# Reordered scans, one projection before the first gates, and turns around the last residual, in an encoder layer

## What is computed

```python
proj = x @ w_in + b_in
u_lru, g_lru, q, k, v, gate_lru, gate_attn = jnp.split(proj, SPLIT_IDX, axis=-1)
u = depthwise_conv(u_lru, w_lru_conv, b_lru_conv, LRU_CONV_PAD)
h_fwd = rg_lru_scan(u, ...)              # forward over positions
h_bwd = flip(rg_lru_scan(flip(u), ...))  # backward
#   r = sigmoid(u @ w_a + b_a), i = sigmoid(u @ w_x + b_x), in 8 blocks of 160 channels
#   a = exp(8 r log_sigmoid(lam)),  h[t] = a[t] h[t-1] + sqrt(1 - a^2) * i * u
y_lru = ((h_fwd + h_bwd) * gelu(g_lru)) @ w_lru_out
y_attn = windowed_gqa(q, k, v, rel_table, attn_sink) @ w_attn_out
mix = (sigmoid(gate_lru) * y_lru + sigmoid(gate_attn) * y_attn) @ w_o + b_o
x = layer_norm(ALPHA * x + mix, ln1_g, ln1_b)
hu = depthwise_conv(x @ w_up + b_up, w_ffn_conv, b_ffn_conv, FFN_CONV_PAD)
val, gt = jnp.split(hu, 2, axis=-1)
return layer_norm(ALPHA * x + (gelu(gt) * val) @ w_down + b_down, ln2_g, ln2_b)
```

## Time and profile before

| | us |
|---|---|
| median of 3 runs (2743.85 to 2744.9) | 2744.3 |
| the profiled execution, whole | 2745.17 |
| its span in the profile | 2743.4 |

### The profile page before, as it was taken

One profiled execution on the slowest core, in us unless ns is written; L12 is line 12 of the kernel. 1 busy time (PEld: TensorE's weight loads), 2 busy tenths in 40 slices (PEclk: granted clock), 3 DMA queues, 4 the chain that ended last, 5 costly groups with the idle time before them and its releaser, 6 DMA issues.

```text
span 2743.4 us, 32010 instructions
## 1 busy us (share of the span) xinstructions
PE 2659.9 (97%) x11898; PEld 2193.1 (80%) x11898; DVE 1486.2 (54%) x1780; ACT 768.5 (28%) x1053; POOL 653.2 (24%) x332
## 2 busy tenths in 40 slices
PE   8998999999999999999999999989999999999998
PEld 6786888888788877888888888878788778888886
DVE  6799754334504568644545464667742414644445
ACT  3565713313400022010101111148932301211112
POOL 3554532232133622434243332310000000000000
PEclk9999999999999999999999999999999999999999
DMA  6554554444596823435343433456656693544554
GB/s 216 198 196 157 200 184 157 173 161 168 201 375 230 314 87 129 157 133 180 129 181 124 177 129 147 148 210 219 227 199 229 218 355 134 207 184 187 198 199 166
DMA packets 168544, 519.94 MB, mean 190 GB/s; under 512 B 13255, under 2 KB 40135, under 8 KB 166384
## 3 DMA queue, kind: packets, MB, share of 16 engines
q1 hardware_dynamic: 113536, 422.02, 42.6%
q10 hardware_dynamic: 54896, 96.39, 9.9%
HBM read 303.13 MB, written 206.32 MB: 186 GB/s over the span
## 4 chain that ended last, share of the span: by engine, by line
PE 83%; DVE 10%; DMA 3%; ACT 3%; issue 1%; SPq 0%; ACTq 0%; DVEq 0%
PE ps L877 49%; PE ps L1218 12%; PE ps L1045 8%; PE ps L1139 4%; PE ps L927 3%; PE ps L1028 2%; PE ps L1078 1%; DMA gate_in<-gate_dram 1%; DMA W<-w_split 1%; PE ps L1065 1%; PE ps L930 1%; PE ps L1207 1%; DVE tau L1801 1%; DVE tau L1791 0%; DVE acc L2082 0%
## 5 line engine op out<-in xcount | busy, mean ns | idle before, releaser
L877 PE MATMUL ps<-XH,W 128*128 128x512 f32 x4224 | 1206.0, 391 | 26.9 <-DVE XL L1746 11.7
L877 PEld LDWEIGHTS ps<-XH,W 128*128 128x128 f32 x4224 | 794.8, 188 | 203.9 <-issue 19.6
L877 PE MATMUL ps<-XL,W 128*128 128x512 f32 x2112 | 710.0, 390 | 0.0
L877 PEld LDWEIGHTS ps<-XL,W 128*128 128x128 f32 x2112 | 397.9, 188 | 82.4
L1218 PE MATMUL ps<-W,HH 128*128 128x512 f32 x1152 | 310.1, 389 | 1.5 <-DVE HL L2065 1.5
L1218 PEld LDWEIGHTS ps<-W,HH 128*128 128x128 f32 x1152 | 216.1, 188 | 46.8 <-DVE HL L2065 1.9
L761 POOL TENSOR_SCALAR W<-raw 128x1024 fp32r<-128x1024 f32 (+2 forms) x72 | 91.4, 1270 | 566.8 <-PE ps L877 301.7
L1045 PE MATMUL ps<-XH,W 128*128 128x512 f32 x672 | 216.4, 393 | 0.0
L827 POOL TENSOR_SCALAR W<-raw 128x1024 fp32r<-128x1024 f32 x72 | 86.8, 1205 | 536.8 <-PE ps L877 228.8
L762 POOL TENSOR_TENSOR W<-raw,W 128x1024 fp32r<-128x1024 f32 (+2 forms) x72 | 205.6, 2855 | 6.0
L828 POOL TENSOR_TENSOR W<-raw,W 128x1024 fp32r<-128x1024 f32 x72 | 190.3, 2643 | 6.0
(11 more groups left out here) (205 smaller groups left out, 3341.8 us busy)
## 6 DMA issues: line engine op xcount, KB each, us to landing
w_split<-W SPq DMA_DIRECT2D x131, 1024.0 KB, 6.2
W<-w_split SPq DMA_DIRECT2D x130, 1024.0 KB, 6.8
raw<-w_mlp SPq DMA_DIRECT2D x72, 512.0 KB, 4.2
raw<-w_qkv_mix SPq DMA_DIRECT2D x28, 512.0 KB, 3.7
w_split<-W SPq DMA_DIRECT2D x8, 1280.0 KB, 12.3
W<-w_split SPq DMA_DIRECT2D x8, 1280.0 KB, 8.3
gate_dram<-mix_out ACTq DMA_DIRECT2D x16, 512.0 KB, 2.7
gate_in<-gate_dram ACTq DMA_DIRECT2D x16, 512.0 KB, 6.2
```

What stands on the lines that cost most here:

```text
L877: last = nc.tensor.matmul(bank(group, c), lhs(wl, k), rhs(xl, k, c), start=(k == 0 and n == 0), stop=(k == nk - 1 and n == 2))
```

## The change

Three places are touched.

**Half.** `decay_steps` is divided (`gate_inputs` and `decay_steps`), and `recur` too (`scans` and `output`). At the transition from half 0 to half 1, DVE now runs: `gate_inputs` and `decay_steps` of (0, REST_TILE), a wait for the sigmoids of block 4, `convolve(1, 1)`, the scans of (0, REST_TILE), `gate_inputs` and `decay_steps` of (1, 0), the split of (1, 1), the scans of (1, 0), then `output(0, REST_TILE)`, `convolve(1, 2)`, `output(1, 0)`. ACT issues the store of (0, REST_TILE) behind the roots and the takes of (1, 0) instead of ahead of its roots. The second square of half 1 goes to `ur[0]` and no longer waits for the moves out of `sig_rest`. A block's first sigmoid waits for one scan instead of two.

**Border.** In `q == 1`, `("g", 0, 0)` comes ahead of `("gates", 0, 0)` in the order of slabs and products; ACT's order of takes stays. The row before the last gets a store semaphore of its own, and ACT waits for the other five only.

**Norm.** Five turns of the first half lie within the last token tile, three between the first parts of `up_half(0, 0)`; the last three take-backs and splits of that half come behind the last tile's norm on ACT and behind its residual on DVE. The products that need them, and the turns of the second half, follow `up_half(1, 0)`'s first five parts.

```diff
-BACK_AT = ((0, 2, 2, 2, 2, 0, 0, 0), (0, 0, 1, 1, 1, 1, 2, 2))
+BACK_AT = (0, 0, 2, 0, 2, 0, 1, 0)
+EARLY_BACK = 5
+TURNS_LATE = (0, 2, 1, 1, 1, 1)
...
+        def order_of(q):
+            return order_lru if q == 0 else order_lru[:3] + [order_lru[4], order_lru[3]] + order_lru[5:]
...
-            return out_stored[0 if tt in (0, SEQS[q] // P - 1) else 1]
+            last = SEQS[q] // P - 1
+            return out_stored[0 if tt in (0, last) else 2 if tt == last - 1 else 1]
...
-            return (sq, sig_rest)[d][:, 0:T]
+            return (sq, ur[0] if h else sig_rest)[d][:, 0:T]
...
-                    for e in order_lru[AHEAD if q else 0:]:
+                    for e in order_of(q)[AHEAD if q else 0:]:
...
                     pe.wait_ge(res_taken[q], nt - 1)
-                    up_half(0, 0)
+                    for k in range(EARLY_BACK):
+                        up_half(0, 0, range(k, k + 1))
+                        if k < KD - EARLY_BACK:
+                            turn_back(0, EARLY_BACK + k)
                     pe.wait_ge(res_taken[q], nt)
-                    up_half(1, 0)
-                    up_half(0, 1).then_inc(slab_done, 1)
-                    up_half(1, 1).then_inc(slab_done, 1)
+                    up_half(1, 0, range(EARLY_BACK))
+                    late = [(n, k) for n in range(2) for k in range(EARLY_BACK, KD)]
+                    made = 0
+                    for (n, k), turns in zip(late, TURNS_LATE):
+                        for kk in range(made, made + turns):
+                            if kk == 0:
+                                pe.wait_ge(normed[q], nt)
+                            turn_back(1, kk)
+                        made += turns
+                        up_half(n, 0, range(k, k + 1))
+                    for kk in range(made, KD):
+                        turn_back(1, kk)
+                    up_half(0, 1, range(KD)).then_inc(slab_done, 1)
+                    up_half(1, 1, range(KD)).then_inc(slab_done, 1)
...
                                 if last is not None:
-                                    act.wait_ge(scan_done[q], 2 * last + 4)
+                                    act.wait_ge(scan_done[q], 2 * last + (4 if m else 3))
...
-                            if h and jj == 0:
-                                store_y(act, q, T, 0, REST_TILE)
                             if h == 0 and jj == HALF - 1:
                                 take("u", 1, REST_TILE)
                             roots(h, jj)
...
                                 for e in behind_gates(h, jj):
                                     take(*e)
+                            if h and jj == 0:
+                                store_y(act, q, T, 0, REST_TILE)
...
                     for tt in range(nt):
                         if tt == nt - 1:
-                            take_back(0)
+                            take_back(0, range(EARLY_BACK))
...
+                    take_back(0, range(EARLY_BACK, KD))
...
+                            r_i = [side(z, jj, T) for z in sig]
+                            if blk == HALF:
+                                output(0, REST_TILE, gelu_gr[:, 0:T])
+                                convolve(1, 2)
+                                output(1, 0, side(gelu_g, 0, T))
+                                continue
...
                         if h == 0:
+                            r_i = [side(z, 0, T) for z in sig]
+                            dve.wait_ge(gate_evac[q], 5 * HALF + 5 + gate_banks(T) - 1)
                             convolve(1, 1)
-                        recur(h, REST_TILE, r_i[0:2], r_i[2:4], gelu_gr[:, 0:T], split_next if h == 0 else (lambda: None))
+                            scans(0, REST_TILE, rests[0:2], rests[2:4])
+                            gate_inputs(1, 0, r_i[2:4], u[0])
+                            decay_steps(1, 0)
+                            split_next()
+                            scans(1, 0, r_i[0:2], r_i[2:4])
...
                         if tt == nt - 1:
-                            split_back(0)
+                            split_back(0, range(EARLY_BACK))
                         add_residual(tt)
-                    split_back(1)
+                    split_back(0, range(EARLY_BACK, KD))
+                    split_back(1, range(KD))
```

More of the change, by code:

```diff
@@ L425, in build @@
         out_ready = PerSeq("out_ready")
-        out_stored = [sem(f"out_stored{i}") for i in range(2)]
+        out_stored = [sem(f"out_stored{i}") for i in range(3)]
         def ln_stat(t):
@@ L697, in _ @@
                 last_gates = None
-                for n, (kind, h, jj) in enumerate(order_lru):
+                for n, (kind, h, jj) in enumerate(order_of(1)):
                     s = first_slab(1, "lru") + n
@@ L908, in gates @@
                     def gates(h, jj):
-                        n = slab_at[("gates", h, jj)]
+                        n = slab_of(q, ("gates", h, jj))
                         blk = HALF * h + jj
@@ L1192, in up, with up_half @@
                         project(n % 2, T, "mlp", n, g=g)
-                    def up_half(n, side):
+                    def up_half(n, side, part):
                         at = side * TH
                         dst = ps[:, 2 * n + at // CH, at % CH:at % CH + TH]
[L1197 to L1204, removed]
+                        if part.start == 0:
+                            slab_in(q, "mlp", n)
+                        for k in part:
                             pe.wait_ge(x1_split[q], KD * side + k + 1)
@@ L1366, in decays @@
                             if d and jj < REST_TILE and not is_short(T):
-                                act.wait_ge(rest_moved[q], 64 * (HALF * h + jj + 2))
-                            A1(square(d, T), r[d], ACT.Square).then_inc(decay_done[q], 1)
+                                if h:
+                                    act.wait_ge(input_gated[q], REST_TILE + 1)
+                                else:
+                                    act.wait_ge(rest_moved[q], 64 * (jj + 2))
+                            A1(square(d, h, jj, T), r[d], ACT.Square).then_inc(decay_done[q], 1)
                     def roots(h, jj):
@@ L1623, in normalise_token_tile, with take_back @@
                            bias=stat[:, 4:5]).then_inc(normed[q], 1)
-                    def take_back(half):
-                        for k in range(KD):
+                    def take_back(half, part):
+                        for k in part:
                             g = half * KD + k
@@ L1686, in _ @@
                     if q + 1 == len(SEQS):
-                        for k in range(2):
+                        for k in range(3):
                             act.wait_ge(out_stored[k], 16 * out_count(q)[k])
@@ L1790, in decay_steps, with scans @@
                             tau_d = tau[n % 2][d][:, 0:T]
-                            tell(V.scalar_tensor_tensor(out=tau_d, in0=square(d, T), scalar=1.0, in1=tau_d, op0=ALU.add, op1=ALU.mult),
-                                 q_ready[q], 2 * n + d + 1)
-                    def recur(h, jj, r, i, gate, between=lambda: None):
+                            tell(V.scalar_tensor_tensor(out=tau_d, in0=square(d, h, jj, T), scalar=1.0, in1=tau_d,
+                                                        op0=ALU.add, op1=ALU.mult), q_ready[q], 2 * n + d + 1)
+                    def scans(h, jj, r, i):
                         n = 5 * h + jj
@@ L1801, in recur, with output @@
                             tell(V.tensor_tensor_scan(o, a, b, 0.0, ALU.mult, ALU.add), scan_done[q], 2 * n + d + 3)
+                    def output(h, jj, gate):
+                        n = 5 * h + jj
+                        tau_j = [t[:, 0:T] for t in tau[n % 2]]
                         order(V.tensor_tensor(tau_j[0], tau_j[0], tau_j[1], ALU.add))
-                        between()
                         dve.wait_ge(proj_evac[q], gelu_at[("g", h, jj)] + 1)
@@ L1834, in _ @@
                                 split_channels(1, REST_TILE)
-                            recur(h, jj, r_i[0:2], r_i[2:4], side(gelu_g, jj, T))
+                            scans(h, jj, r_i[0:2], r_i[2:4])
+                            output(h, jj, side(gelu_g, jj, T))
                             if jj < HALF - 1 and blk + 2 < BLOCKS:
@@ L2015, in add_residual, with split_back @@
                         scale_and_shift(ln_stat(tt % 4), norm_ready[q], tt + 1)
-                    def split_back(half):
+                    def split_back(half, part):
                         at = slice(half * TH, (half + 1) * TH)
-                        for k in range(KD):
+                        for k in part:
                             g = half * KD + k
```

50 lines of the change are left out of this document (29 added, 21 removed).

## The result

| | before | after |
|---|---|---|
| median of 14 runs each, us | 2744.94 (2743.85 to 2748.33) | 2751.39 (2747.26 to 2754.89) |
| the profiled execution, whole | 2745.17 | 2748.74 |
| its span | 2743.4 | 2746.9 |

The ratio is 1.0021, with a 95% interval of 1.0014 to 1.0028: about 6 us slower by these times, clear of the interval but small. The forecast was 2746.3, its range 2737 to 2752. The same kernel in a later set of runs gave 2748.85 against 2745.28, ratio 1.0014 (1.0005 to 1.0023), or 3.6 us slower.

The account below looks back on a forecast made before the run. PE was taken to bound the kernel, at work 2660 of 2743.4 us. Terms -1.1 + 2.4 - 4.8 - 2.7 + 0.9 = -5.3, plus clock +7.3, gave +2.0 on 2744.3: 2746.3 us, range 2737 to 2752.

Parts of the forecast that it names:

- Rival 1: All places: the found waits don't bind and the change does what its order suggests; -27, 2717 us; chance 0.12.
- Rival 2: New waits: PE's clock doesn't fall behind waits of 4 to 5 us; -5.3, 2739.0 us; chance 0.15.
- rival 3: New waits: clock falls behind all four as long as at the border, 2.8 each; +5.9, 2750.2 us; chance 0.15.
- Half, first sequence: Wait before block 5's first sigmoid: PE resumes at 243.5 to 245.5 against 245.59; gain 0.1 to 2.1, taken -1.1.
- The value of the one-scan wait: Half, first sequence: the looser wait for one scan is worth nothing behind the store of y(0, REST).
- Border: Start of second sequence: u_stack moves ready earlier, PE then waits 4.8 us for a gelu before g(0, REST); -4.8.
- the 9.9 that the filled gap was said to promise: Border: gain promised by the filled gap and its clock, where the forecast took -4.8 instead.
- Norm, first: First sequence's norm: residual starts 4.6 earlier, but turn 7 waits 6.0 us for an ACT take; -2.7 (-3.6 to -0.6).
- t + 8.3: First norm: when turn 7 of the second half comes, t being its first turn; part of POOL's split still falls there.
- Norm, second: Second sequence's norm: turn 7 waits 4.3 us in place of 1.65; +0.9 (0.5 to 1.2).
- Half, second: Second sequence's half: PE resumes at 1939.3 instead of 1936.90, with a new wait of 4.2 us; +2.4.
- The clock's total: Behind four new waits: low PE clock costs 1.5 for three and 2.8 for the 6.0 us one; +7.3, bounds 0 and 11.2.

Follow-up runs that it names:

- three moves: Changed kernel with y(0, REST)'s store behind block 5's sigmoids, turn 7 behind the second half's first five parts, second sequence's first gelu taken before the gates' sigmoids; 2728.24 us.
- norm alone: Kernel before with only the norm's part of the change; 2746.51 us against 2745.28, ratio 1.0002.
- border alone: Kernel before with only the border's part of the change; 2746.97 us against 2745.28, ratio 1.0006.
- turn late: Changed kernel with turn 7 of the norm's first half moved behind the first five parts of the second; 2746.24 us against 2745.22 for before.
- half alone: Kernel before with only the half's new order; 2749.37 us against 2745.28, ratio 1.0017.
- moves first: Three moves, with SP's fetch of the second sequence's sixth slab held until the moves into u_stack have landed; 2727.23 us against 2745.31 for before.
- store behind: Changed kernel with ACT's store of y(0, REST) moved from behind block 4 to behind block 5's four sigmoids; 2738.82 us against 2745.22 for before.
- both scans: Store behind, with the first sigmoid again waiting for both scans of the block before instead of one; 2742.50 us against 2745.00 for before.
- no own semaphore: Three moves, without the semaphore of its own for the last row but one; 2728.69 us against 2745.31 for before.
- norm out: Three moves, with the norm's part as in the kernel before; 2731.07 us against 2745.31 for before.

## Why the prediction was right, and where it was not

The time lies inside the range, 5.1 over the forecast by the first median and 2.5 by the second. By the trace it is closer still, +3.5 against +2.0, but in part by luck: the places that the sum names came out 4.2 us above it together, and what it doesn't name took 2.7 back. The mechanism was read rightly at all five places: the half keeps its wait with the store right ahead of the table load; g(0, REST) waits 4.7 (predicted 4.8); turn 7 waits 5.5 and 4.2 (6.0 and 4.3); the second half waits 3.7 and resumes at 1939.18 (1939.3). Rival 1, that the waits don't bind, falls with them. Rival 2, no clock, falls in this execution, in which all four windows are low; rival 3, 11.2 us for them, was too much by 3, though its time, 2750.2, is nearer the first median than the forecast is. What was mis-sized, term by term:

- **Half, first sequence**, -1.1 against +1.1. PE resumes at 245.25, in before's time 246.0 (this kernel began 0.8 us early), behind the upper end of 245.5. The scans end at 239.52, also 0.8 early, so at 240.3: the upper end of 238.2 to 240.2. POOL's subtraction held one DVE operation, as in the earlier trace rows: the scan that began at 231.57 ended 2.15 us behind it, of its own 2.29. That is the Trainium skill's rule in SBUF — State Buffer, section "SBUF: two separate sides", by which the two exclude each other for a whole instruction; the trace agrees, and with it the end at 240.2 was the one to take, not the middle. The issue of the store, about 0.35 of ACT's queue, was counted in the second sequence and forgotten in the first. And the clock behind this wait, 1.9 us lost before and 2.6 now, had no term at all.
- **The value of the one-scan wait.** "Worth nothing behind it" was right, as the store stood; what followed from it, that moving one store a few instructions down is worth 10 us, was not drawn.
- **Border**, -4.8 + 1.5 against -0.1. The take started 1.7 earlier and not 2.35. Then the moves into u_stack: the forecast had PE's gates follow the projection at 1836.1, and they began at 1838.14 behind a DMA. ACT now issues the moves while SP's weight fetches are in flight; that this slows them is what the run with the held fetch shows, in the version with the three moves. The clock took 2.4, not 1.5. The moves, a start of the last wait 0.2 later, and the clock make 2.0 + 0.2 + 0.9 = 3.1 of the 3.2 missed. And the 9.9 that the filled gap was said to promise is 9.6 by its own rows (1855.8 - 1846.2), which changes no term.
- **Norm, first**, -2.7 + 2.8 against -1.3. The clock is right to the tenth (2.8). The turns of the second half end 7.2 us after the first (t + 8.3 taken), since none of POOL's subtractions fell there: the third ended at 1029.28, 2.4 before the first of these turns.
- **Norm, second**, +0.9 + 1.5 against +2.3: right to 0.1, term by term. PE went on at 2335.61, in before's time 2334.3, as forecast; the eight parts behind took 1.6 us more than at full speed; and from the second half's first turn (2340.25) to the end it was 10.95, where 11.0 was taken. The clock loss came through whole, as it did in the second execution (+2.4).
- **Half, second**, +2.4 + 1.5 against +4.2: right within 0.3. The 4.2 us taken for its wait is not worked out in the forecast: from the old start, 1936.90 - 2.56, to 1939.3 it would be 5.0. It measured 3.73, since PE stopped later.
- **Not in the sum**: the start, -0.8 and -1.3 in the two executions of the changed kernel, attention 1, +0.8 in both, and attention 2, -2.6 and -3.0. The last was put at nothing since no instruction changes there.

The clock's total, +7.3 for four waits, was near the 8.0 measured, but as a sum of unequal errors. The rule of TensorE: Matmul & The Clock Gate, section "HAM oscillation — how this bites in real kernels", in the Trainium skill, that waits between groups of matmuls bring the array back at half clock each time, fits all four. Behind shorter waits, at the second half, the rows of this case show both: 1.00 behind 2.56 us (before) and 2.54 (norm alone), 0.51 behind 2.57 (border alone).

**What stays open.** In the first set of 14 runs the median is 6.4 over before, the profiled execution only 3.6, and single times reach 2754.9; in the second set they reach 2752.7. The profile is of one execution, and no profile here is of a time above 2750. What differs between the profiles at places that have the same code is the clock behind a wait and the length of attention 2, both below; that they make the spread of the times too is not shown. Why attention 1 is 0.5 to 0.8 longer in every kernel with the new half (2.2 in turn late) was not tried.

## What to carry over

When an operation is moved later on one engine, look up what waits for its result on the others, and what is queued behind that wait: a store that costs 0.33 us to issue held ACT, and through it PE, for 6 us. A freed wait is worth something only down to the next one in the same queue, so write out all the waits at a place before counting a gain, and move the blocking ones together: the three small moves turned a change that costs 4 to 6 us into one that wins 17. Count the clock behind each new wait as well: at the changed kernel's second norm all of it came through.

## What the chip showed beyond that

**The clock is not a function of the wait.** Waits of 2.57 and 2.56 us in the same place were followed by granted clocks of 0.51 and 1.00; the half's wait of 11.6 us in the first sequence by 0.53 over 5.5 us in the changed kernel and 0.74 in turn late, whose code there is the same. That is 1.2 us, and all of the difference between their first halves in the table.

**Attention 2 differs by up to 4.6 us with no instruction changed.** From 1950 to 2316 us of before the kernels took from 4.1 us less to 0.5 us more. It is not a give-back of what was gained ahead of it: of the kernels that came to it 5 to 17 us early, some kept its length (three moves, moves first) and some made it 1 to 3 us shorter (store behind, both scans, no own semaphore, norm out). Part of the difference is the clock. The same wait in before and in the half alone, each with the 5 us behind its first microsecond:

```profile
1982.06 0.50 PE L877 MATMUL ps<-XH,W 128*128 128x512 f32 x1 [1.96 <-ACT gelu_g L1332]
```

```profile
1983.00:1988.00 5.00, 5.00 (x17) 0.66 0.34 141
```

```profile
1989.16 0.50 PE L884 MATMUL ps<-XH,W 128*128 128x512 f32 x1 [1.96 <-ACT gelu_g L1339]
```

```profile
1990.00:1995.00 5.00, 5.00 (x24) 1.00 0.36 147
```

That makes 1.5 us of the half alone's 4.1. Another part lies about the y_attn products, where PE's waits for `z_kept` are 5.6 us in before and between 4.0 (norm out) and 6.6 (turn late) in the others, and the DMA engines are 0.90 to 0.95 busy. Whether the weight fetches set these waits was not tried.
